# Constant products ahead of TensorE's waits in three attention loops of a two-model kernel

## The reference

```python
# layer 0: block-sparse attention (8 heads) and selected/window attention (8 heads), head size 64
p = masked_softmax(concat([s_sel, s_own]) * scale, ok)         # causal within one block of 256
o_moba = einsum('bhqj,bhjd->bhqd', p, v)
p_c = masked_softmax(einsum('bgrqd,bgnd->bgrqn', qg, kc) * scale, ok_c)   # kc, vc: compressed keys
o = g[..., 0:1] * o_c + g[..., 1:2] * o_s + g[..., 2:3] * o_w
# layer 1: differential attention, 8 heads, two maps each, value size 128
a = p[:, :, 0] - lam * p[:, :, 1]
o = rms_norm(einsum('bhqk,bhkd->bhqd', a, v), out_norm) * (1.0 - lam_init)
# second model, attention over 256 context and 256 latent tokens, 8 query heads, 4 kv heads, size 128
p = softmax(einsum("bqkgd,bskd->bkgqs", qg, k) * HEAD_DIM_2 ** -0.5)
o = einsum("bkgqs,bskd->bqkgd", p, v)
```

## Time and profile before

| | |
|---|---|
| time, three runs | median 1711.74 us (1711.67 to 1712.48) |
| the profiled execution | 1709.29 us, its span 1707.2 us |
| mean granted clock of TensorE | 0.941 |
| busy share of the span | PE 91%, PEld 77%, DVE 55%, ACT 42%, POOL 0% |
| the chain that ended last | PE 79%, DVE 14%, ACT 2%, issue 2%, DMA 2% |
| loop 0 | 139.3 to 217.3 us of the span |
| loop 1 | 556.4 to 596.1 us |
| loop 3 | 1427.5 to 1474.2 us |

### The profile page before, as it was taken

The page is one execution under the profiler, slowest core; times in us unless marked ns, Lnnn a source line. Parts: engine busy times, 40 slices in busy tenths (PEclk is TensorE's granted clock), DMA queues, the critical chain, the costliest instruction groups (busy, mean ns, idle before and its releaser), DMA issues.

```text
span 1707.2 us, 24515 instructions
## 1 busy us (share of the span) xinstructions
PE 1549.2 (91%) x10326; PEld 1308.6 (77%) x10326; DVE 938.3 (55%) x1609; ACT 718.6 (42%) x1098; POOL 0.2 (0%) x4
## 2 busy tenths in 40 slices
PE   3998789999898789999979999799998886999997
PEld 2766668898686559888759988688986764779986
DVE  3584545345669755334575455753456786363455
ACT  2353524334444424333435544344444543345543
POOL 0000000000000000000000000000000000000000
PEclk9997789999998889999979999899999898989999
DMA  9962157965544657997734655469655353545552
GB/s 370 368 240 99 50 173 266 306 201 178 185 149 157 213 173 251 306 306 254 241 111 151 195 174 190 142 210 305 205 195 172 124 172 123 173 124 177 171 195 86
DMA packets 165845, 336.42 MB, mean 197 GB/s; under 512 B 8160, under 2 KB 109160, under 8 KB 165480
## 3 DMA queue, kind: packets, MB, share of 16 engines
q1 hardware_dynamic: 138880, 230.90, 40.2%
q10 hardware_dynamic: 26856, 103.96, 18.0%
HBM read 333.79 MB, written 1.05 MB: 196 GB/s over the span
## 4 chain that ended last, share of the span: by engine, by line
PE 79%; DVE 14%; ACT 2%; issue 2%; DMA 2%; ACTq 0%; SPq 0%; DVEq 0%
PE ps L1584 22%; PE ps L1585 21%; PE ps L1586 21%; PE ps L1556 5%; DVE wlo L945 2%; PE ps L1715 2%; DVE res L1024 1%; DVE work L1022 1%; PE ps L1712 1%; PE ps L1812 1%; PE ps L1785 1%; ACT whi L556 1%; PE ps L1824 1%; DVE work L1109 1%; PE ps L1754 1%
## 5 line engine op out<-in xcount | busy, mean ns | idle before, releaser
L945 DVE TENSOR_TENSOR wlo<-wraw,whi 128x1024 fp32r<-128x1024 f32 (+1 forms) x424 | 498.1, 1216 | 415.1 <-ACT whi L556 414.6
L556 ACT ACTIVATE whi<-wraw 128x1024 fp32r<-128x1024 f32 (+1 forms) x424 | 423.7, 1047 | 472.5 <-PE ps L1586 452.6
L1584 PE MATMUL ps<-hT_hi,whi 128*128 128x256 f32 x1472 | 422.5, 287 | 0.0
L1585 PE MATMUL ps<-hT_lo,whi 128*128 128x256 f32 x1472 | 416.9, 283 | 0.0
L1586 PE MATMUL ps<-hT_hi,wlo 128*128 128x256 f32 x1472 | 416.5, 283 | 0.0
L1584 PEld LDWEIGHTS ps<-hT_hi,whi 128*128 128x128 f32 x1472 | 282.8, 192 | 20.2 <-issue 18.1
L1585 PEld LDWEIGHTS ps<-hT_lo,whi 128*128 128x128 f32 x1472 | 282.9, 192 | 0.0
L1586 PEld LDWEIGHTS ps<-hT_hi,wlo 128*128 128x128 f32 x1472 | 282.8, 192 | 0.0
L1584 PE MATMUL ps<-whi,act_hi 128*128 128x512 f32 x560 | 219.0, 391 | 0.0
L1585 PE MATMUL ps<-wlo,act_hi 128*128 128x512 f32 x560 | 218.1, 390 | 0.0
L1586 PE MATMUL ps<-whi,act_lo 128*128 128x512 f32 x560 | 217.9, 389 | 0.0
(11 more groups left out here) (200 smaller groups left out, 1319.6 us busy)
## 6 DMA issues: line engine op xcount, KB each, us to landing
wraw<-in_mlp_w_dram SPq DMA_DIRECT2D x96, 1024.0 KB, 5.4
ring<-in_ada_w_dram ACTq DMA_DIRECT2D x90, 1024.0 KB, 5.6
wraw<-in_ffn_w_gate_dram SPq DMA_DIRECT2D x22, 1024.0 KB, 6.2
wraw<-in_ffn_w_up_dram SPq DMA_DIRECT2D x22, 1024.0 KB, 6.2
wraw<-in_ffn_w_down_dram SPq DMA_DIRECT2D x22, 1024.0 KB, 4.9
wraw<-in_diff_w_in_dram SPq DMA_DIRECT2D x12, 1024.0 KB, 5.0
wraw<-in_attn_w_qkv_dram SPq DMA_DIRECT2D x12, 1024.0 KB, 5.1
wraw<-in_sp_w_in_dram SPq DMA_DIRECT2D x8, 1024.0 KB, 13.0
```

The costliest lines, as they stand in the source:

```text
L556: nc.scalar.activation(whi[:, u % 2, part], raw_view(u)[:, part], ACT.Copy).then_inc(hi_ready, 1)
L945: nc.vector.tensor_tensor(wlo[:, u % 2, part], raw_view(u)[:, part], whi[:, u % 2, part].bitcast(F32), ALU.subtract).then_inc(lo_ready, 1)
L1584: mm(dst, s_hi, m_hi, start=start, stop=False, skip_group_check=skip)
L1585: mm(dst, s_hi, m_lo, start=False, stop=False, skip_group_check=skip)
```

## The change

Ahead of `turn` two products of the constant tiles are run, and ahead of `values` one (loop 0) or two (loops 1 and 3). They multiply `half_r` (128 columns) by all of `causal_r` (512 columns) in fp32r and write a whole PSUM bank: the bank that the following transposes or products overwrite. To be allowed to write there they stand behind the wait that frees the bank (`pT` of the step before in `turn`, `taken` in `values`), and the wait for the step's own data (`exps` or `mixed`, and `pT`) now comes after them.

```diff
+                def idle_products(bank, many):
+
+                    for _ in range(many):
+                        mm(ps[:, bank, :], half_r[:, 0:P], causal_r[:, :, :, :].rearrange("p h b n -> p (h b n)"), start=True, stop=True, skip_group_check=True)
+
                 def turn(i):
-                    pe.wait_ge(a.mixed if stage == 1 else a.exps, i + 1)
                     if stage == 1:
                         if i >= 2:
                             pe.wait_ge(a.pT, i - 1)
@@ -1807,15 +1811,18 @@
                         if i >= 1:
                             pe.wait_ge(a.pT, i)
                         maps = [(4 + m, a.p[:, i % 2, m, :]) for m in range(2)]
+                    idle_products(maps[0][0], 2)
+                    pe.wait_ge(a.mixed if stage == 1 else a.exps, i + 1)
                     for bank, src in maps:
                         for b in range(a.width // P):
                             ins = nc.tensor.transpose(ps[:, bank, b * P:(b + 1) * P], src[:, b * P:(b + 1) * P], ident)
                     ins.then_inc(a.turned, 1)
 
                 def values(i):
-                    pe.wait_ge(a.pT, i + 1)
                     if i >= 1:
                         pe.wait_ge(a.taken, i)
+                    idle_products(6, 1 if stage == 0 else 2)
+                    pe.wait_ge(a.pT, i + 1)
                     if stage == 3:
```

## The result

The changed kernel is slower: 1717.81 us (median of five runs, 1716.98 to 1720.05) against 1711.67 (1706.56 to 1712.48), ratio 1.0041 with a 95% interval of 1.0028 to 1.0055. Its profiled execution took 1716.98 us with a span of 1715.2, 8.0 longer than before. Run twice more beside other kernels it gave 1.0012 (1.0000 to 1.0024) and 1.0017 (1.0008 to 1.0027). A copy of the kernel before gave 1.0016 (1.0008 to 1.0025), though it should give 1. So a ratio here is good to about 0.2%, whatever its interval says. Over all rounds the changed kernel took 1716.0 us on average (27 runs) and the kernel before 1711.8 (75 runs, without the twelve of the copy): +4.2 us, 0.25%. The two later ratios are no larger than the copy's.

A forecast was written before the change was run, and what follows sets the result against it. TensorE bounds loop 3, VectorE paces loop 1, and loop 0's TensorE runs at clock 0.75 with waits. 8.8 + 4.9 + 1.0 = 14.7 us on 1709.29 gives 1724.0, plus 2.45 for the median: 1726 us, range 1722 to 1731.

The forecast's parts named there:

- The order of the waits: Loops 0 and 3: the copy ends last, so products behind its wait run after the gap and do not fill it.
- The clock's term for loop 0: Loop 0: a clock that stays up or returns sooner gives back 5.6 us, of at most 20.2.
- the length of the gap ahead of a low stretch: Loop 0: the clock fell behind a 1.47 us gap, not behind 0.47 and 0.32; shortening it to 0.56 gives back 3.4 us.
- the price of a product: All three loops, full clock: 0.34 us for the first or a single product, 0.23 for one following, 0.57 a pair.
- forecast 8.8: Loop 3: 16 pairs at 0.57 cost 9.1 us, less a 0.3 us wait; bounds 7.1 and 10.6.
- forecast +4.9: Loop 0: 14.6 us of products, less 4.1 in waits, leaves 10.5; less 5.6 from the clock; bounds -16.0 and +12.2.
- forecast +1.0: Loop 1: +0.7 in steady iterations, +1.1 for two pairs at the end, -0.8 from the clock; bounds -1.5 and +3.5.
- my 0.8 us: End of loop 1: pairs shorten two long waits and may keep the clock up there, giving back 0.8 us.
- the forecast of +14.7: Whole kernel: loop 3's 8.8, loop 0's 4.9 and loop 1's 1.0 us add up to 14.7 us slower.
- the rival with cheap products: All three loops: products at the low price, clock as forecast, +8.8 us in sum, 1720.5 us; chance 0.2.
- The rival in which the clock holds all through loop 0: Loop 0: low stretches vanish, the loop costs -13.4 us, the sum is -4.4, 1707 us, faster; chance 0.05.
- the rival in between: Loop 0's clock gives back 11 to some 15 us, products at low price: -3.7 to about 0, 1710 to 1715; chance 0.08.

The follow-up runs named there:

- the loop-1 run: The added products in loop 1 alone (2 and 2), loops 0 and 3 as in the kernel before; ratio 0.9987 against the kernel before.
- the added tails: Products into a free scores bank, in gaps behind loop 0's steps and behind loop 1; without products inside any steps, 0.9957 against the kernel before.
- the two runs that have products in its steps and its gaps: One kernel run twice: the change in loops 0 and 1, loop 3 as before, plus products in the gaps; 0.9925 and 0.9951 against the kernel before.

## Why the prediction was too high

**What held.** The order of the waits: the products stand behind the wait for line 722 in loop 0. Loop 3 is bound by TensorE and pays for every product; nothing came back there. In loop 1 the first pair fits into the wait. The clock's term for loop 0 had about the right size: forecast 5.6 us; TensorE's busy time in the low stretches fell from 40.5 to 25.2 us, and half of the difference is 7.7. That was luck in part. I took the length of the gap ahead of a low stretch for its cause; in the trace after, and in loop 0 of the loop-1 run, gaps of 1.39, 1.59 and 2.07 us passed at full clock, and of the three stretches that went I had named one.

**The step that failed is the price of a product.** I read the distance from the first fp32r product to the second behind loop 3, 0.34 us, as what the first one costs. It is the distance of two starts, and it leaves out how soon the group ahead is followed: in loop 3 the scores after 1.42 instead of 1.82 us. In loop 3 the measured price is 0.227 us for each, the first included, by the iterations of 5.58, 6.49 and 7.42 us. In the other loops it is a little higher: two iterations of loop 0 at full clock without a wait took 3.19 us before (169.39 to 172.58) and 3.94 after (168.17 to 172.11), 0.75 for three products where I had taken 0.91; there the pair does add 0.57, and the single one behind the transposes only 0.18. With these prices the terms become:

- loop 3: 32 x 0.227 = 7.3 less the waits at the end; measured +6.55 to the transposes and +6.9 to the end of the kernel, forecast 8.8;
- loop 0: 12 x 0.75 = 9.0, at the clock of 0.83 that it really had 10.8; less 3.6 covered and 7.7 from the clock, -0.5; measured -0.85 to the transposes and -1.6 to the projection behind them, in the first trace; forecast +4.9. In the second and third trace it is +1.0 to the projection, and the same program varies by 4 us here, so this sum is no proof, and the size of the term is open within that. I had also priced the products at the old clock of 0.75 while giving the clock back beside it;
- loop 1: forecast +1.0, measured -2.4, of which 1.0 us is given back up to the projection and 1.2 more up to loop 3, so that -0.2 is left. In place of my 0.8 us the clock stayed up from 564 to 568 us and in the last steps, where it had been low from 591.7. TensorE needs 4.22 us for an iteration with the products (572.14 to 576.36, the starts of two pairs), hardly more than VectorE's 4.10.

The price alone (7.3 for 9.1 in loop 3, 9.0 for 10.9 in loop 0, about 1 us in loop 1) takes the forecast of +14.7 to some +9, which is the rival with cheap products (its own sum gave 1720.5). That rival is nearest, at a measured 1717.8 and over all rounds 1716.0. The 3 to 5 us that are still missing lie in loops 0 and 1, where I forecast a cost of 5.9 us; the traces show none that stands out of their scatter. The rival in which the clock holds all through loop 0 did not come: the 17 us behind it stayed, since no product stood in its gaps. For this stretch the added tails show the cause. Inside the loop low stretches stayed even with them: its mean clock was 0.85 and 0.89 in the two runs that have products in its steps and its gaps. One slip in the sums: the rival in between, at -3.7 us, begins at 1708 and not at 1710.

## What to carry to other kernels

In this kernel the added products raised the clock for certain only where they could start while the engine waits: look for the wait that ends last and for a place to write that does not hang on that same wait, here a bank of the scores instead of the bank that the copy is about to free. (The kernels with tails also have more products, and the same number behind the wait was not tried.) Where the engine is busy and at full clock, as in loop 3, each such product costs its full price; leave that loop alone. Price a piece of inserted work by the length of a whole iteration with and without it, not by the distance between two starts. Follow a gain past the end of the stretch in which it appears: loop 1's 2.4 us were nearly gone by the next loop.

## What the runs showed of the hardware

A program with the same instructions took 74.0 to 78.0 us for loop 0, depending on where the low stretches of the clock fell on it, and a copy of a kernel measured 0.16% slower than itself. A change of the clock in one place moves the low stretches behind it: loop 1's products lifted the clock in the loop from 0.90 to 1.00, and 2.2 of the 2.4 us were given back before loop 3. A gap's length did not decide by itself whether the clock fell behind it: it did behind one of 1.47 us (before) and did not behind one of 2.07 (after). An fp32r product of 512 columns between the fp32 products of loop 3 cost no more than in a row of its own kind, 0.227 us; in loop 0 three of them cost 0.75.
